# Moving the middle projection units and the turns of x in a one-core streaming encoder step

## What is computed

```python
p = rms_norm(x) @ w_in                 # 2304 columns: q, k, v of 8 stick-breaking heads; q, k, v of the window heads
o_sb = stick_breaking(q_sb, k_sb, v_sb)                # all earlier keys, blocks of 128
o_sw = sink_window_attention(q_sw, k_sw, v_sw)         # window of 128, ALiBi, sinks
h = x + concat(rms_norm(o_sb), rms_norm(o_sw)) @ w_out
q = (rms_norm(h) @ w_q).reshape(t, 8, 2, 128)          # 8 heads of product keys
v1, i1 = top_k(q[..., 0, :] @ keys_1.T, 16); v2, i2 = top_k(q[..., 1, :] @ keys_2.T, 16)
best, pos = top_k(v1[:, None] + v2[None], 16)          # 16 of 256 candidates, expert id = i1 * 128 + i2
y = sum_k softmax(best)_k * gelu(u[id_k] . xn) * v[id_k]   # 128 experts for each token
out = rms_norm(h + y)
```

## Time and profile before

| what | us |
|---|---|
| median of 3 runs | 3173.43 |
| lowest and highest | 3172.75, 3174.1 |
| the profiled execution | 3165.28 |
| its span | 3163.4 |
| busy: PE, DVE, POOL, ACT | 2237.8, 2204.5, 1544.9, 1539.9 |
| first gather issued | 166.03 |

### The profile page before, as it was taken

The page is one execution under the profiler, slowest core; times in us unless marked ns, Lnnn a source line. Parts: engine busy times, 40 slices in busy tenths (PEclk is TensorE's granted clock), DMA queues, the critical chain, the costliest instruction groups (busy, mean ns, idle before and its releaser), DMA issues.

```text
span 3163.4 us, 42434 instructions
## 1 busy us (share of the span) xinstructions
PE 2237.8 (71%) x12346; PEld 1128.1 (36%) x12346; DVE 2204.5 (70%) x5717; ACT 1539.9 (49%) x3399; POOL 1544.9 (49%) x1596
## 2 busy tenths in 40 slices
PE   7978788688767756766577657767677666767663
PEld 4755334344333322332243223332333234432220
DVE  3268548684677767786777766786777767686886
ACT  2235325452257425753476337752677347753222
POOL 0034455354544555455555554455554644466553
PEclk9989889789877867887688778887788877767675
DMA  8379999899999999999999999999999999999997
GB/s 326 95 289 411 417 400 416 322 407 383 421 420 373 417 422 397 363 417 416 420 378 354 417 425 359 364 419 421 394 373 366 423 389 406 406 393 417 426 425 299
DMA packets 243623, 1216.73 MB, mean 385 GB/s; under 512 B 30528, under 2 KB 90304, under 8 KB 107200
## 3 DMA queue, kind: packets, MB, share of 16 engines
q0 software_dynamic: 152528, 1108.81, 85.4%
q1 hardware_dynamic: 90864, 105.22, 9.6%
HBM read 1197.56 MB, written 16.47 MB: 384 GB/s over the span
## 4 chain that ended last, share of the span: by engine, by line
DMA 30%; PE 27%; DVE 20%; issue 8%; DVEq 5%; ACT 3%; POOL 2%; ACTq 2%; SPq 0%; another core or an unknown queue 0%; POOLq 0%
DMA r_uv<-peer_uv,f_idx 27%; DVE r_uv L1195 8%; PE f_y_acc L1733 6%; PE f_q_ps L1668 4%; PE f_z L1627 3%; PE f_z L1485 3%; POOL r_uv L975 2%; PE f_z L1492 2%; PE f_y_acc L1594 2%; PE f_z L1465 2%; ACTq L1119 2%; DMA f_work<-w_out 1%; PE f_o_sb L1512 1%; PE f_o_sw L1654 1%; ACT f_diag L1121 1%
## 5 line engine op out<-in xcount | busy, mean ns | idle before, releaser
L975 POOL DMA_INDIRECT r_uv<-peer_uv,f_idx x1056 | 1270.1, 1203 | 1358.7 <-PE f_y_acc L1733 960.7
L1195 DVE CUSTOM_DVE_ANT_0 r_uv<-r_uv,r_x_rep 128x1024 f32<-128x1024 f32 x1056 | 1287.4, 1226 | 521.0 <-DMA r_uv<-peer_uv,f_idx 511.4
L1733 PE MATMUL f_y_acc<-r_uv,f_diag 128*32 128x512 f32 x4224 | 722.4, 760 | 689.7 <-ACT f_diag L1121 684.5
L1115 ACT ACTIVATE f_act_hid<-f_hid 128x2 f32<-128x2 f32 x528 | 107.3, 203 | 942.7 <-DVE f_hid L1195 916.2
L1733 PEld LDWEIGHTS f_y_acc<-r_uv,f_diag 128*32 128x32 f32 x4224 | 94.7, 119 | 972.1 <-ACT f_diag L1121 893.9
L988 ACT ACT_TABLE_LOAD x191 | 245.1, 1283 | 235.3 <-PE f_z L1465 168.7
L961 POOL TENSOR_TENSOR f_gate_fold<-r_fold,f_gates 128x64 f32<-128x64 f32 x528 | 269.0, 509 | 172.7 <-ACT f_diag L1121 157.3
L1115 ACT ACT_TABLE_LOAD x259 | 332.3, 1283 | 4.5
L1668 PE MATMUL f_q_ps<-r_w_q,f_xnT 128*128 128x256 f32 x1152 | 322.8, 429 | 9.7 <-ACT f_xnT L1084 5.8
L1121 ACT ACTIVATE f_diag<-f_gate_fold,f_act_hid 128x32 f32<-128x32 f32 x1056 | 281.9, 314 | 37.9 <-issue 1.7
L1668 PEld LDWEIGHTS f_q_ps<-r_w_q,f_xnT 128*128 128x128 f32 x1152 | 236.3, 214 | 101.1 <-issue 43.0
(11 more groups left out here) (209 smaller groups left out, 2964.2 us busy)
## 6 DMA issues: line engine op xcount, KB each, us to landing
r_uv<-peer_uv,f_idx POOLq DMA_INDIRECT x1056
f_work<-scratch_projT SPq DMA_DIRECT2D x86, 128.0 KB
r_w_out<-w_blocks SPq DMA_DIRECT2D x36, 256.0 KB
f_work<-out_sb_v_prompt SPq DMA_DIRECT2D x72, 128.0 KB
r_uv<-w_blocks SPq DMA_DIRECT2D x16, 512.0 KB, 11.0
r_w_q<-w_peer_q SPq DMA_DIRECT2D x8, 1024.0 KB, 10.6
x_in<-x_prompt SPq DMA_DIRECT2D x8, 512.0 KB, 10.0
f_q_pad<-scratch_projT SPq DMA_DIRECT2D x64, 64.0 KB
```

The source lines that it names most:

```text
L975: pool.indirect_dma_start(uv[:, n % RING, :], None, io["peer_uv"], bass.IndirectOffsetOnAxis(ap=idx[:, head, k:k + 1], axis=0),).then_inc( ...
L1115: nc.scalar.activation(act_hid[:, batch % 4, :], hid[:, batch % 8, :], ACT.Gelu)
L1195: nc.vector.tensor_tensor_reduce(row_u, row_u, x_rep[:, g % 3, :], 1.0, 0.0, ALU.mult, ALU.add, hid[:, n // 2 % 8, n % 2:n % 2 + 1]).then_ ...
L1733: last = nc.tensor.matmul(y_acc[quarter, g % 2 * 512:(g % 2 + 1) * 512], diag[:, batch % 3, i, :], uv[:, n % RING, DM + b * 512:DM + (b + ...
```

## The change

Five things are edited.

1. **Last block out of the ring.** The chunks of the first part are now 4, 4, 4, 3 and 3 blocks; blocks 15 to 17 go to the three buffers of x_rep (w_triple), blocks 0 to 14 to the ring. The second half of xnT_middle moves from x_rep to g_final, and the scratch for the squares from g_final to w_late, for which load_late waits for all squares. The last chunk has scaled and unscaled blocks, so rows_out uses two ACTIVATEs, and two blocks of it are turned.
2. **x turns moved up by one step** in PE's order of the first part: turn_x(3) to turn_x(7) each stand one half projection earlier, turn_rows(3) and turn_rows(4) come together ahead of turn_x(8). On ACT normalise(5) goes ahead of rows_out(2) and normalise(8) ahead of rows_out(4); on DVE stage_out(1) goes behind normalise(5), and stage_out(3) and stage_out(4) behind normalise(8) and scale_turned(7).
3. **Middle units placed anew.** The first eight start at slot -93 instead of -85, two of them ahead of the first scores. Block 15 is now the ninth unit and block 17 the last; the units behind move to later slots (10 to 17: -34, -30, -20, -11, -7, -3, 1, 11), and late units 18 to 36 follow.
4. **The holds** follow: gather 7 waits for 17 units instead of 18, ACT's copies of x for the units of blocks 15 to 17, the third copy of x moves from slots 12 and 16 to 20 and 24, and the first w_out row that is streamed into g_final waits for the middle units.
5. **Second queries of tile 0 behind the keys.** POOL zeroes q_pad in two halves with a semaphore step each; SP waits for the first half, loads two query pieces and the keys of step 0, then waits for the second half and loads the other two.

```diff
-CHUNKS = ((4, 4), (0, 4), (8, 4), (12, 4), (16, 2))
+C_TRIPLE = 15
+CHUNKS = ((4, 4), (0, 4), (8, 4), (12, 3), (C_TRIPLE, 3))
...
-    r.xnT_middle = [half.rearrange("p (k t) -> p k t", k=DK // 2) for half in (r.y[:, 1, :], r.x_rep[:, 2, :])]
+    r.xnT_middle = [half.rearrange("p (k t) -> p k t", k=DK // 2) for half in (r.y[:, 1, :], r.g_final[:])]
...
-    r.w_pair = r.x_rep[:, 0:2, :].rearrange("p c (k n) -> p c k n", k=DK)
+    r.w_triple = r.x_rep[:].rearrange("p c (k n) -> p c k n", k=DK)
...
-RING_PLACE = {**{c: c - 4 for c in range(4, 8)}, **{c: c + 4 for c in range(4)}, **{c: c for c in range(8, 16)}}
+RING_PLACE = {**{c: c - 4 for c in range(4, 8)}, **{c: c + 4 for c in range(4)}, **{c: c for c in range(8, C_TRIPLE)}}
...
-        squares = r.g_final
+        squares = r.w_late[:, 0:2, :, :].rearrange("p s k n -> p (s k n)")
...
+            sp.wait_ge(s_sq, len(ORDER))
             for p in range(3):
                 load_late(sp, io, r, p)
...
@@ scalar
+                scaled = sum(column_scale(b) != 1 for b in range(c, c + n)) * P
+                if 0 < scaled < n * P:
+                    nc.scalar.activation(rows[:, j, 0:scaled], acc[j % 4][:, 0:scaled], ACT.Copy, scale=SCALE)
+                    last = nc.scalar.activation(rows[:, j, scaled:n * P], acc[j % 4][:, scaled:n * P], ACT.Copy)
...
             normalise(4)
+            normalise(5)
             rows_out(2)
-            normalise(5)
             normalise(6)
             rows_out(3)
             normalise(7)
+            normalise(8)
             rows_out(4)
-            normalise(8)
@@ vector
             normalise(4)
-            stage_out(1)
             scale_turned(3)
             normalise(5)
+            stage_out(1)
             scale_turned(4)
             normalise(6)
             scale_turned(5)
             normalise(7)
             scale_turned(6)
+            normalise(8)
+            scale_turned(7)
             stage_out(3)
-            scale_turned(7)
             stage_out(4)
-            normalise(8)
             scale_turned(8)
@@ tensor
             project(2, 0)
+            turn_x(3)
             project(2, 1)
             turn_rows(1)
-            turn_x(3)
+            turn_x(4)
             project(3, 0)
-            turn_x(4)
+            turn_x(5)
             project(3, 1)
-            turn_x(5)
+            turn_x(6)
             project(4, 0)
-            turn_x(6)
+            turn_x(7)
             project(4, 1)
             turn_rows(3)
-            turn_x(7)
             turn_rows(4)
             turn_x(8)
...
-MIDDLE_ORDER = [4, 5, 6, 7, 0, 1, 2, 3, 17, 16, 8, 9, 10, 11, 12, 13, 14, 15]
+MIDDLE_ORDER = [4, 5, 6, 7, 0, 1, 2, 3, 15, 16, 8, 9, 10, 11, 12, 13, 14, 17]
...
-MIDDLE_SLOT = [*(FIRST_SLOT + 8 + 4 * i for i in range(8)), -52, -47, -34, -30, -25, -19, -14, -8, 0, 5]
-LATE_SLOT = [*MIDDLE_SLOT, 10, 18, 22, 26, 32, 42, 50, 54, 58, 62, 66, 70, 76, 82, 87, 92, 100, 105, 109, 114, 131, 145, 155, 160,
-             165, 173, 177, 181, 185, 189, 193, 197, 201, 205, 209, 213]
+MIDDLE_SLOT = [*(FIRST_SLOT + 4 * i for i in range(8)), -52, -47, -34, -30, -20, -11, -7, -3, 1, 11]
+LATE_SLOT = [*MIDDLE_SLOT, 18, 26, 30, 34, 42, 50, 54, 58, 62, 66, 70, 74, 78, 82, 86, 90, 94, 102, 106, 114, 131, 145, 155,
+             160, 165, 173, 177, 181, 185, 189, 193, 197, 201, 205, 209, 213]
...
-LATE_PLACE = [BANKS[a] for a in "yY" * 8 + "wb" + "sswswsswsbwbwbwbbwbwwsswbbwbsbwbwbwb"]
+LATE_PLACE = [BANKS[a] for a in "yY" * 8 + "wb" + "sswssswsbwbwbwbwbbwwwsswbbwbsbwbwbwb"]
...
-X_FIRST = [-10, -5, 12, 60, 98, 126, 168, 188]
+X_FIRST = [-10, -5, 20, 60, 98, 126, 168, 188]
...
+            def load_second_q():
+                hold(sync, S["zeroed"], 2)
+                load_q(0, 1, 2)
...
                     hold(sync, S["y_out"], t - 1)
+                else:
+                    hold(sync, S["late_mm"], N_MIDDLE)
...
                     load_k(*at)
+                    if at == (0, 0):
+                        load_second_q()
...
-            nc.gpsimd.memset(q_pad[:], 0.0).then_inc(S["zeroed"], 1)
+            for f in range(2):
+                nc.gpsimd.memset(q_pad[:, f, :, :, :], 0.0).then_inc(S["zeroed"], 1)
...
-                    hold(pool, S["late_mm"], 2 * n + (2 if n < RING // 2 else 4))
+                    hold(pool, S["late_mm"], 2 * n + 2 if n < RING // 2 else min(2 * n + 4, N_MIDDLE - 1))
...
-                    act.wait_ge(S["late_mm"], N_MIDDLE if g == 2 else MIDDLE_ORDER.index(C_KVSW) + 1)
+                    act.wait_ge(S["late_mm"], MIDDLE_ORDER.index(C_TRIPLE + g) + 1)
```

25 lines of the change are left out of this document (12 added, 13 removed).

## The result

| | before | changed |
|---|---|---|
| median, us | 3163.51 (16 runs) | 3177.73 (16 runs) |
| ratio to before, 95% | | 1.0043 (1.0027 to 1.0059) |
| profiled execution, its span | 3165.28, 3163.4 | 3171.25, 3169.5 |

The change makes the kernel slower by 0.43%, some 14 us. The forecast of a gain of 11.3 us had the wrong sign, and 3177.73 lies above all of its range.

The account below looks back on a forecast made before the run. The prediction took idle DMA, or the time before the first gather, to bound the kernel. Terms 2.4 - 1.2 - 1.5 - 11.0 = -11.3 us gave 3162.1 us against the median of 3173.43; range 3149 to 3176, the forecast's own 3155 to 3167.

Parts of the forecast that it names:

- What bounds the kernel: Whole kernel: DMA is busy nearly everywhere, so idle DMA or the time before the first gather moves the end.
- The absolute time: Whole kernel: forecast 3162.1 us, taken against the median of 3173.43 us.
- First part: Up to the second part's opening: x turns moved up make POOL's last store later, +2.4 us (ends +1.0 and +4.3).
- Start of the second part: Opening through windows to merged rows' turn: two units moved ahead save PE time, partly returned as waiting, -1.2 us.
- Up to the first gather: First queries through select to first gather: fewer pairs and turns on PE, -1.5 us (ends 0 and -2.2).
- The clock: PE's thinned places: idle gaps of 2.0 to 2.3 us keep 2.4 GHz; otherwise up to 4.5 us more.
- Gap (a): DMA idle from 188 to 202 us, behind the first gathers: eighth gather goes out 20 us behind first, -11.0 us.
- After that: Units 17 to 35 and their DMAs move a few slots; PE has room there, so 0 us.
- Rival 4: Slots 60 to 125: moved late units delay key or w_out loads, 9.6 us per wait, slower with two; chance 0.13.
- Rival 1: Gap (b) closes as well, as a natural store leaves the spot ahead of tile 2's key load: 3152.5 us; chance 0.15.
- gap (b): DMA share 0.40 from 566 to 582 us, 9.6 us idle, where PE waits 10.8 us for tile 2's keys.

Follow-up runs that it names:

- e7: Kernel before with only the late units at their new slots and banks, and X turn of the third group at slot 20; 3184.04 us, ratio 1.0073.
- e12: Kernel before with the late units' natural stores issued on SP 11 slots behind their unit instead of 8; 3152.10 us, ratio 0.9976.
- e17: Changed kernel with the units' natural stores issued by ACT ten slots behind their unit instead of by SP eight behind; 3159.94 us, ratio 1.0003.
- e4: Changed kernel with the late units' slots and the first part's order on PE, ACT and DVE both back as before; 3161.18 us, ratio 0.9994.
- e5: e4 with the first eight middle units also back at their old slots, none ahead of the first scores; 3156.81 us, ratio 0.9984.
- e1: Changed kernel with the last middle unit at slot 5, late units at their old slots and banks, X turn at slot 12; 3163.77 us, ratio 0.9995.
- e3: Changed kernel with a late unit's weights load put ahead of the window load of the same slot on SP; 3179.06 us, ratio 1.0036.
- e9: Changed kernel with two late units moved, from slot 102 to 103 and from 106 to 109; 3177.51 us, ratio 1.0058.
- e13: Changed kernel with the four query loads of tile 2 sent at slot 95 instead of 103; 3181.01 us, ratio 1.0057.
- e15: Changed kernel with the natural key stores of blocks 4 to 7 cut to one row each, some 2,700 rows fewer; 3176.01 us, ratio 1.0042.
- e16: Changed kernel with the changes of e13 and e15 at once; 3158.23 us, ratio 1.0008.
- e11: e5 with natural stores three slots later on SP and the eighth and later first gathers waiting for all 18 middle units; 3155.50 us, ratio 0.9989.

## Why the prediction was wrong

- **What bounds the kernel**: right for DMA left idle, which moved the end wherever a run made or closed such a gap (e7, e12, e17). For the time before the first gather it is not shown: the 5.3 us between e4 and e5 had shrunk to 1.3 by gather 160.
- **The absolute time**: 3162.1 was worked out from a median of three runs that stood 10 us over that of all 16. With the sum right it would have come out near 3152, below the forecast's own 3155 to 3167.
- **First part, +2.4 (ends +1.0, +4.3)**: measured +5.2 (67.91 for 62.72), outside its ends. The stores went out as worked out (59.79 for 60.2), but I took 3.8 us to land, since I had the last w_q loads "nearly over by then". They were not: DMA stood at 0.93 to 1.01 from 58 to 68 us, and the store took 7.0. The x loads did go out 3.9 us sooner (the last at 40.14 for 44.01), but the small loads that follow took SP until 54.9, up to 3 us each to issue, so the last three w_q loads went out at 54.95, half a microsecond later than before. The store itself was 128 KB where the one of the earlier trace rows was 64; which of the two made it slow is open.
- **Start of the second part, -1.2**: wrong in sign. Scores began 9.6 us after the opening, as worked out (9.7 to 10.4), but the merged turn came 1.3 us later, not earlier (55.2 us after the opening for 53.9). What the two units had freed in the windows was not taken up: the turns came at 98.06, 101.95, 106.52 and 109.03, only the last pair under 3 us apart, and PE then idled 2.8 us in 14 at a granted clock of 0.76. The pairs of traces above put the two units at 3 to 5 us.
- **Up to the first gather, -1.5**: from the merged turn on, -1.5 in this trace. First gather at 170.98, not 165.7. Six more traces with the same first part and start (e1, e3, e9, e13, e15, e16) had it at 172.8 to 175.7; why the profiled execution was quicker is open, and that its lag is 5 us and not 7 to 10 is luck.
- **The clock**: by the Trainium skill (TensorE: Matmul & The Clock Gate, Part 1) idling puts the array back at half rate. The trace agrees in one of three thinned places: 0.76 in the 14 us from 109.2, where the same stretch had 1.00 before; from 123 to 171 us it stayed at 1.00. No single idle time of PE in those 14 us was over 1.56 us, so comparing the length of one gap with 2.50 and 3.03 us, by which I had kept 2.4 GHz, was a wrong reading of the earlier trace rows. By that rule, with the 1.5 us that I had worked out for one place, the start would have come to +0.3, which has the right sign; measured was +1.3.
- **Gap (a), -11.0**: right in mechanism, and -11.5 from gather 4 to gather 8. That the size fits is in part luck, since the trace of before had the gap 4 to 5 us wider than e7 and e12, and of DVE's 12.6 us of waiting 9.8 were the gap's. (From the select to the first gather the rows give 1.55 us, not 1.75, which changes nothing here.) What it is worth at the end is less, some 6 us (e11).
- **After that, 0**: this is the step that failed, by more than the whole gain. "PE has room there... Their DMAs move too", and then I followed the stores, queries, keys and the third copy, but not the units' own weights. The room on PE was itself the trouble: it passes the four slots between the load's release and its use in 7.7 to 8.8 us, for a landing of 19.5 to 24.9. I took slots for a fixed time, and the 2.88 us that PE waited at 516.28 in the kernel before, the sign that this lead was already used up, I had not looked at. It cost 10.7 and 17.3 us of waiting, and each time 15 us in the gathers. What made the second one land late is its own queue, with rows of 512 B ahead of it (e13 and e17); why the first took 19.5 us is open (e3, e17); the keys of the earlier trace rows had the stores in front of them too (e12).
- **Rival 4** (0.13) was the case that came. Its mechanism was near (SP's loads too late under full DMA through the moved late units), its count right (two waits); the place was half right (slots 30 and 106; 60 to 125 was named), the wait stood at weights, not at keys or w_out, and its price of 9.6 us was too small. Against it I had set that "the ring of eight gathers, some 20 us, covers short waits"; here the cover was 10 and 15 us and used up when PE came back, and the gathers started late behind that, with PE at the 0.50 level.
- **Rival 1**: gap (b) did close, but its 10.6 us paid for part of this.
